# Layer-1 output products as seven block products of eight, and GpSimd work in instructions of 256 columns

## The reference, cut to what matters

```
h = rmsnorm(x) * (1 + scale) + shift
u, z = split(h @ w_in)                       # 1024 -> 2 x 2048
mixed = einsum(mean over windows of u - u, w_grp) * pool_scale   # four groups of 512 channels
y = (mixed * silu(z)) @ w_out                # 2048 -> 1024
x = x + gate * y
```

## Time and profile before

| | us |
|---|---|
| three runs | 1632.49, 1634.61, 1634.99 |
| median | 1634.61 |
| profiled execution | 1636.07 |
| its span, first to last instruction | 1633.3 |

### The profile page before, as it was taken

How to read it: one execution, slowest core, us unless ns; L and a number is a source line. 1 busy time by engine, 2 the same in 40 slices (tenths; PEclk the granted TensorE clock), 3 DMA queues, 4 the chain that set the end, 5 groups by cost and what they waited for, 6 DMA issues and landing times.

```text
span 1633.3 us, 24914 instructions
## 1 busy us (share of the span) xinstructions
PE 1594.1 (98%) x9703; PEld 1483.3 (91%) x9703; DVE 832.8 (51%) x1314; ACT 457.9 (28%) x969; POOL 377.0 (23%) x385
## 2 busy tenths in 40 slices
PE   6999999999999999998999999999999999999996
PEld 4899999999999999997888898888998989989896
DVE  4653549354854466448424563245623456234565
ACT  4321112110211011124416404064140542214423
POOL 3021222121221112111314213042231331314310
PEclk8999999999999999998999999999999999999998
DMA  9512221221122212210202212012120231201312
GB/s 335 194 56 78 68 57 54 67 79 55 56 67 67 67 56 62 84 41 28 65 14 72 91 41 78 13 61 89 50 68 14 65 97 41 66 25 40 110 38 110
DMA packets 137544, 115.01 MB, mean 70 GB/s; under 512 B 6013, under 2 KB 120281, under 8 KB 137442
## 3 DMA queue, kind: packets, MB, share of 16 engines
q1 hardware_dynamic: 135616, 112.87, 22.4%
q10 hardware_dynamic: 1834, 0.74, 0.2%
HBM read 99.05 MB, written 15.00 MB: 70 GB/s over the span
## 4 chain that ended last, share of the span: by engine, by line
PE 94%; DVE 3%; SPq 1%; DMA 1%; ACT 1%; issue 0%; ACTq 0%; DVEq 0%
PE psA L587 40%; PE psB L587 29%; PE psB L1857 7%; PE psA L1857 4%; PE psB L1914 2%; PE psB L1931 2%; PE psB L1922 2%; PE psX L1951 1%; PE psX L1896 1%; DVE a_hi L675 1%; PE psB L1963 1%; DVE y_rows L1650 1%; PE psX L1764 1%; DMA ada<-in_ada_w 1%; PE psB L1964 0%
## 5 line engine op out<-in xcount | busy, mean ns | idle before, releaser
L355 POOL TENSOR_TENSOR w_lo<-stage,w_hi 128x1024 fp32r<-128x1024 f32 x100 | 249.5, 2495 | 884.8 <-ACT w_hi L350 884.8
L350 ACT ACTIVATE w_hi<-stage 128x1024 fp32r<-128x1024 f32 x100 | 107.0, 1070 | 426.5 <-PE psB L587 297.5
L587 PE MATMUL psA<-h_hi,w_hi 128*128 128x362 f32 (+1 forms) x864 | 210.9, 349 | 5.1 <-DVE h_lo L491 4.8
L587 PE MATMUL psA<-h_lo,w_hi 128*128 128x362 f32 (+1 forms) x864 | 193.8, 329 | 0.0
L587 PE MATMUL psA<-h_hi,w_lo 128*128 128x362 f32 (+1 forms) x864 | 193.6, 329 | 0.0
L587 PEld LDWEIGHTS psA<-h_hi,w_hi 128*128 128x128 f32 x864 | 151.8, 191 | 28.1 <-issue 22.3
L587 PEld LDWEIGHTS psA<-h_lo,w_hi 128*128 128x128 f32 x864 | 151.9, 190 | 0.0
L587 PEld LDWEIGHTS psA<-h_hi,w_lo 128*128 128x128 f32 x864 | 151.7, 190 | 0.0
L587 PE MATMUL psA<-a_hi,w_hi 128*128 128x362 f32 (+1 forms) x480 | 109.6, 334 | 2.5 <-DVE a_lo L678 1.3
L587 PE MATMUL psB<-h_hi,w_hi 128*128 128x362 f32 (+1 forms) x480 | 109.6, 331 | 0.0
L587 PE MATMUL psB<-h_hi,w_lo 128*128 128x362 f32 (+1 forms) x480 | 107.8, 327 | 0.0
(11 more groups left out here) (364 smaller groups left out, 2767.9 us busy)
## 6 DMA issues: line engine op xcount, KB each, us to landing
stage<-in_gla_w_in SPq DMA_DIRECT2D x40, 512.0 KB, 3.6
stage<-in_pool_w_in SPq DMA_DIRECT2D x32, 512.0 KB, 3.9
ada_stage<-in_ada_w SPq DMA_DIRECT2D x24, 512.0 KB, 4.0
ada<-in_ada_w SPq DMA_DIRECT2D x16, 512.0 KB, 7.8
stage<-in_pool_w_out SPq DMA_DIRECT2D x16, 512.0 KB, 3.3
v<-in_state_gla SPq DMA_DIRECT2D x32, 256.0 KB, 2.6
out_new_gla_sample<-v SPq DMA_DIRECT2D x32, 256.0 KB, 2.1
stage<-in_gla_w_out SPq DMA_DIRECT2D x16, 512.0 KB, 3.4
```

What stands on the lines that cost most here:

```text
L350: nc.scalar.activation(slot_hi(plan, j), stage[:, j % 2, :], ACT.Copy).then_inc(lay.hi_done, 1)
L355: nc.gpsimd.tensor_tensor(slot_lo(plan, j), stage[:, j % 2, :], slot_hi(plan, j).bitcast(f32), ALU.subtract).then_inc(lay.lo_done, 1)
L587: last = nc.tensor.matmul(ps[u][:, t, 0:width], weight(w[:, p, :], k), a[:, k, n0:n0 + width], start=(k == 0 and pas == 0), stop=(k == kt ...
```

## The change

A slot's output product is a product of blocks: two halves of the tokens (544 columns each, `H0` and `H1`), two pairs of input tiles, two output tiles. Eight block products before; the change makes them from seven (Winograd's form), for O23, O45 and O67 in groups 0 to 2 and O23 and O45 in group 3. O01, and O67 of group 3, stay as they are.

- TensorE (`project_seven`): seven products of 12 matmuls (2 input tiles x 3 passes x 2 column parts of 272). Four of them take mixed operands, and some accumulate onto the result of an earlier one: 1, 3, 5 and 7 in one PSUM region of two banks, 4 and 6 in another, 2 alone. VectorE reads a region between two products that add to it, so TensorE waits for these reads.
- VectorE (`sum_tiles`, `sums_low`, `add_seven`): per group, eight sums of 544-column tiles for the mixed activations, four of them ahead of the gating of the last tile and four behind it, and eight low parts of them; per slot, seven additions of PSUM to `xT` in place of two.
- ScalarE (`sums_high`, `weights_high`): eight high parts of the sums per group, and four of 256 columns of the mixed weights per slot. Three of the sums' high parts stand ahead of the last silu.
- GpSimd (`weights_mixed`): per slot four mixed weight quarters, made in place in `stage`, and their four low parts, each of 256 columns in two strips of 128. Every low part of a slot, in both layers, is now four instructions of 256 columns in place of one of 1024. The low part of O23 waits until all activations of O01 are split (`act_part`).
- Loads: as `stage` is now read and rewritten after a slot's low part is done, O67's load waits for O23's product, and the first two loads of the next group for O45's and O67's. The mixed weights' high parts lie in `ada_stage`, so the load of the first adaLN columns of groups 1 to 3 moves behind that of slot 1. The mixed activations lie in `oT` (low), `PQ`, `G` and `SZ` (high).
- Ends: ScalarE's and GpSimd's loops end one group earlier and the last group is written out. The squares for the norm of layer 2 wait until O45 of group 3 is done, and the small weight copy `w_gl_hl` moves behind six of the seven whole squares.
- A few semaphores are merged (`ident_ready`, `copied`, `gate_ready`, the halves of `ada0_loaded` from the third on).

```diff
         def lo_slots(lay, plan, eng, g, j):
             eng.wait_ge(lay.hi_done, g * plan.slots + j + 1)
-            nc.gpsimd.tensor_tensor(slot_lo(plan, j), stage[:, j % 2, :], slot_hi(plan, j).bitcast(f32),
-                                    ALU.subtract).then_inc(lay.lo_done, 1)
+            if plan is PP and PP.names[j] == "O23":
+                eng.wait_ge(act_part, g * 3 + 3)
+            for n in range(0, D, D // 4):
+                c = slice(n, n + D // 4)
+                last = nc.gpsimd.tensor_tensor(slot_lo(plan, j)[:, c], stage[:, j % 2, c],
+                                               slot_hi(plan, j)[:, c].bitcast(f32), ALU.subtract)
+            last.then_inc(lay.lo_done, 1)
...
+        def project_seven(pe, g, name):
...
+            def multiply(out, i, h, mixed, a_high, a_low, first):
+                wh = mixed_quad(g, name, i, h) if mixed else quad(whi, i, h)
+                wl = quad(mlo if mixed else wlo, i, h)
+                for k in range(2):
+                    for pas, (w, x) in enumerate(((wh, a_high), (wh, a_low), (wl, a_high))):
+                        for n in range(2):
+                            last = nc.tensor.matmul(acc[out][n], w[:, k, :], x[:, k, n * (half // 2):(n + 1) * (half // 2)],
...
+            if name == "O23":
+                pe.wait_ge(L0.evac[0], g * PP.in_set[0] + PP.place[u] + 1)
...
+            slot_ready(pe, L0, PP, g, name)
+            multiply(a, 0, 0, False, a_hi[:, 0:2, H0], a_lo[:, 0:2, H0], True).then_inc(seventh_done, 1)
+            if name != "O23":
+                pe.wait_ge(seventh_read, read - 7 + 6)
+            multiply(b, 1, 0, False, a_hi[:, 2:4, H0], a_lo[:, 2:4, H0], True).then_inc(seventh_done, 1)
+            pe.wait_ge(mix_w_low, 8 * no + 5)
+            pe.wait_ge(mix_a_lo, 4 * g + 2)
+            pe.wait_ge(seventh_read, read + 1)
+            multiply(a, 1, 1, True, mix_a[1], alo[1], False).then_inc(seventh_done, 1)
...
+            pe.wait_ge(mix_w_low, 8 * no + 6)
+            multiply(c, 0, 0, True, mix_a[0], alo[0], True).then_inc(seventh_done, 1)
+            pe.wait_ge(mix_w_low, 8 * no + 7)
+            pe.wait_ge(mix_a_lo, 4 * g + 4)
+            pe.wait_ge(seventh_read, read + 3)
+            multiply(a, 0, 1, True, mix_a[2], alo[2], False).then_inc(seventh_done, 1)
+            pe.wait_ge(seventh_read, read + 4)
+            multiply(c, 1, 1, False, mix_a[3], alo[3], False).then_inc(seventh_done, 1)
+            pe.wait_ge(mix_w_low, 8 * no + 8)
+            pe.wait_ge(seventh_read, read + 5)
+            multiply(a, 1, 0, True, a_hi[:, 2:4, H1], a_lo[:, 2:4, H1], False).then_inc(L0.unit_done, 2)
...
+        def sum_tiles(dve, k, chain):
...
+            link(nc.vector.tensor_tensor(oT[:, 2 + k, H1], oT[:, k, H1], oT[:, 2 + k, H1], ALU.add))
+            nc.vector.tensor_tensor(oT[:, k, H1], oT[:, k, H0], oT[:, k, H1], ALU.subtract)
+            link(nc.vector.tensor_tensor(oT[:, k, H0], oT[:, 2 + k, H1], oT[:, k, H0], ALU.subtract))
+            nc.vector.tensor_tensor(oT[:, 2 + k, H0], oT[:, 2 + k, H0], oT[:, k, H0],
+                                    ALU.subtract).then_inc(mix_a_sum, 1)
+        mix_steps = {1: [(0, 0), (1, 0), (2, 0)], 2: [(0, 1), (1, 1)], 3: [(3, 0), (3, 1)], 4: [(2, 1)]}
...
+        def weights_mixed(pool, g, name):
...
+            pool.wait_ge(L0.lo_done, g * PP.slots + j + 3)
+            nc.gpsimd.tensor_tensor(quad(w, 0, 0), quad(w, 0, 1), quad(w, 0, 0), ALU.subtract).then_inc(mix_w_low, 1)
+            nc.gpsimd.tensor_tensor(quad(w, 0, 1), quad(w, 1, 1), quad(w, 0, 1), ALU.subtract).then_inc(mix_w_low, 1)
+            pool.wait_ge(mix_w_low, 8 * no + 2)
+            nc.gpsimd.tensor_tensor(quad(w, 1, 1), quad(w, 1, 1), quad(w, 0, 0), ALU.subtract).then_inc(mix_w_low, 1)
+            pool.wait_ge(mix_w_low, 8 * no + 3)
+            nc.gpsimd.tensor_tensor(quad(w, 1, 0), quad(w, 1, 0), quad(w, 1, 1), ALU.subtract).then_inc(mix_w_low, 1)
+            for n, (i, h) in enumerate(mix_order):
+                pool.wait_ge(mix_w_hi, 4 * no + n + 1)
+                nc.gpsimd.tensor_tensor(quad(mix_wl[:, j % 2, :], i, h), quad(w, i, h),
+                                        mixed_quad(g, name, i, h).bitcast(f32), ALU.subtract).then_inc(mix_w_low, 1)
...
+        def add_seven(dve, g, name, mod, chain, last_group):
...
+            dve.wait_ge(seventh_done, 6 * no + 1)
+            add_first(a, m).then_inc(seventh_read, 1)
...
+            add_first(b, m).then_inc(seventh_read, 1)
+            if name == "O23":
+                sums_low(dve, g, 4)
...
                     slot_free(L0, PP, g, j, sp)
+                    if j in (0, 1) and not first:
+                        wait_apart(sp, L0.unit_done, units(PP, g, 2 * j - 2))
+                    if j == PP.slot["O67"]:
+                        wait_apart(sp, L0.unit_done, units(PP, g, PP.unit["O23"] + 2))
...
+                    if name == "Z3":
+                        sums_high(act, g, 1)
                     if name[0] == "Z":
                         silu_out(act, L0, PP, g, int(name[1]))
                     if j + 2 < PP.slots:
                         split_slot(L0, PP, act, g, j + 2)
                     if j in extra:
                         extra[j]()
+                    if name == "Z3":
+                        for step in (2, 3, 4):
+                            sums_high(act, g, step)
+                        weights_high(act, g, "O23")
...
+            act.wait_ge(L0.unit_done, units(PP, NG, -2))
+            nc.scalar.activation(x_cols[:, NSUP + 1:NSUP + 2], eps[:], ACT.Sqrt)
+            squares_between(act)
             act.wait_ge(wgl_loaded, 16)
             nc.scalar.activation(w_gl_hl[:, :, 0:RANK], w_gl[:], ACT.Copy).then_inc(wgl_hi, 1)
-            nc.scalar.activation(x_cols[:, NSUP + 1:NSUP + 2], eps[:], ACT.Sqrt)
-            squares_between(act)
             squares_last(act)
...
                         gate_tile(dve, L0, PP, g, i, chain)
-                for name in ("O01", "O23", "O45"):
-                    add_branch(dve, L0, PP, g, name, mods[0], chain, last_group)
+                    if i == KG - 2:
+                        sum_tiles(dve, 0, chain)
+                        sums_low(dve, g, 1)
+                sum_tiles(dve, 1, chain)
+                add_branch(dve, L0, PP, g, "O01", mods[0], chain, last_group, (0,))
+                sums_low(dve, g, 2)
+                sums_low(dve, g, 3)
+                add_branch(dve, L0, PP, g, "O01", mods[0], chain, last_group, (1,))
+                add_seven(dve, g, "O23", mods[0], chain, last_group)
+                add_seven(dve, g, "O45", mods[0], chain, last_group)
```

More of the change, by code:

```diff
@@ L603, in w4, with quad, sevens, seven_no @@
             return lambda w, k: w[:, k * 256 + half * P:k * 256 + half * P + P]
+        def quad(w, i, h):
+            return w.rearrange("p (k h m) -> p k h m", k=KG, h=2)[:, 2 * i:2 * i + 2, h, :]
+        def sevens(g):
+            return ("O23", "O45") if isinstance(g, int) and g == NG - 1 else ("O23", "O45", "O67")
+        def seven_no(g, name):
+            return g * 3 + ("O23", "O45", "O67").index(name)
+        def seven_acc(g, name):
+            if isinstance(g, int) and g == NG - 1:
+                return {"O23": (1, 0, 2), "O45": (2, 0, 1)}[name]
+            return {"O23": (0, 1, 2), "O45": (1, 2, 0), "O67": (2, 0, 1)}[name]
@@ new lines, in mixed_quad @@
+        def mixed_quad(g, name, i, h):
+            last_group = isinstance(g, int) and g == NG - 1
+            return mix_w5[1 if name == "O45" and not last_group else 0][:, i, :, h, :]
+        def project_seven(pe, g, name):
+            u, p, no = PP.unit[name], PP.slot[name] % 2, seven_no(g, name)
+            a, b, c = seven_acc(g, name)
+            read = 7 * no
+            whi, wlo = w_hi[:, p, :], w_lo[:, p, :]
+            mlo, alo = mix_wl[:, p, :], mix_al
+            def multiply(out, i, h, mixed, a_high, a_low, first):
[5 more added lines that the diff above has]
+                            last = nc.tensor.matmul(acc[out][n], w[:, k, :], x[:, k, n * (half // 2):(n + 1) * (half // 2)],
+                                                    start=(first and k == 0 and pas == 0), stop=(k == 1 and pas == 2),
+                                                    skip_group_check=True)
+                return last
+            if name == "O23":
+                pe.wait_ge(L0.evac[0], g * PP.in_set[0] + PP.place[u] + 1)
+            else:
+                pe.wait_ge(seventh_read, read - 7 + (6 if seven_acc(g, name) == (2, 0, 1) and g == NG - 1 else 2))
+            slot_ready(pe, L0, PP, g, name)
[8 more added lines that the diff above has]
+            if name == "O23":
+                pe.wait_ge(L0.evac[1], g * PP.in_set[1] + PP.place[u + 1] + 1)
+            else:
+                pe.wait_ge(seventh_read, read)
+            pe.wait_ge(mix_w_low, 8 * no + 6)
[9 more added lines that the diff above has]
```

(29 more changed lines are left out.)

156 lines of the change are left out of this document (135 added, 21 removed).

## The result

The changed kernel takes 1641.46 us in the median of six runs (1638.05 to 1642.83), the kernel before 1634.40 in six (1632.49 to 1635.18): a ratio of 1.0043, interval 1.0032 to 1.0053. It is **7.1 us slower**; 9.4 us faster had been forecast. The profiled execution took 1638.93 us with a span of 1637.1, so 3.8 us of span more than before.

The account below looks back on a forecast made before the run. TensorE, busy 98% of the span, was taken as the bound. Gains of 15.9 and 4.4 less losses of 10.0 and 0.9 gave 9.4 us: median 1625.2 us, own range 1619 to 1631, 8 in 10 within 1614 to 1636.

Parts of the forecast that it names:

- Part 1: TensorE in eleven output slots: seven products of 272-column matmuls, slot 10.49 us against 11.93; 15.9 us gained.
- Part 2: Gating of the last tile: GpSimd held back, VectorE's conversion falls from 2.58 to 0.35 us; 4.4 us gained.
- Part 3: VectorE between O01 and product 3 of O23: TensorE stalls 2.5 us in each of four groups; 10.0 us lost.
- six meetings of ten: Between O01 and product 3: six of ten two-SBUF-operand VectorE instructions find a GpSimd piece in flight, about 0.55 us each.
- the 0.8 of room: VectorE's slack before product 3 of O23 without meetings: 0.2 us at the end and 0.6 idle before.
- Rival (b): In front of product 3 the granted clock falls in the stall: four falls, 6.8 us, 1632; chance 0.17.
- (d): Strict alternation of VectorE and GpSimd before product 3: stall 4.7 us a group, 8.8 more, 1634; chance 0.10.
- Rival (c): GpSimd becomes the bound from gating's end to U0, at 1.2 us a piece: slower, 1646; chance 0.09.
- Part 4: Rest of a slot: VectorE's reads, ScalarE's copies and GpSimd's other slots find cover; nothing gained or lost.
- Some 8 us ahead: GpSimd's other slots, 0.5 us longer each in pieces, were to end this far ahead of TensorE.
- Part 5: Weights that load later (O67, next group's U0): 8.3 us from slot end, under 10.5; nothing lost.
- part 6: End of layer 1: squares start behind O45's end and finish late; about 0.9 us lost, 0 to 2.

Follow-up runs that it names:

- e7: Changed kernel without the wait that holds GpSimd's low part of O23 until O01's activations are split: 1636.05 us, ratio 1.0016.
- e3: Changed kernel with 32 more matmuls of 240 columns behind product 2 of O23, into an unused bank, filling the stall: 1632.25 us, ratio 0.9995.
- e4: Changed kernel with O23 as eight products again, so only O45 and O67 run as seven, none in group 3: 1624.58 us, ratio 0.9948.
- e11: Changed kernel with every low part of a weight slot as one GpSimd instruction of 1024 columns, mixed weights still in pieces: 1635.81 us, ratio 1.0008.
- e5: Changed kernel with three of VectorE's eight low parts of the sums moved behind the read that releases product 3 of O23: 1629.21 us, ratio 0.9974.
- e6: Changed kernel with GpSimd's low part of O23 held until VectorE's four sums behind the gating are done: 1625.00 us, ratio 0.9939.
- e9: Changed kernel with O23's GpSimd low part held for the four sums and three sums' low parts behind product 3's releasing read: 1624.72 us, ratio 0.9946.
- e10: As e9, with the low parts of U0 to U3 as one GpSimd instruction of 1024 columns each: 1622.87 us, ratio 0.9928.

## Why the prediction was wrong

**Part 1 (right).** Pairs of 272-column matmuls start 0.25 us apart, 0.125 each (0.1243 forecast, bounds 0.1215 to 0.127). The slots without the stall are 10.61 on average, 10.49 forecast.

**Part 2 (right as far as it went).** O01's first half is 6.07 us instead of 7.17 in every group: 1.1 x 4, as forecast, and the work ahead of the gating fitted. That the held GpSimd work must then fall on the sums was in the prediction; that not holding it would have been cheaper was not (e7).

**Part 3 (the step that failed).** The place, the wait and the mechanism were right: product 3, VectorE as releaser, its row behind GpSimd's pieces. The term that was mis-sized is what the meetings cost: "I take six meetings of ten", 3.3 us in all. All ten met a piece, and that made 4.7 us in group 1. The four sums took 4.8 us (2.9 counted), the four low parts 4.75 (2.7), the two halves of O01 2.3 and 2.1 (1.8 each). A meeting cost 0.47 us, less than the 0.55 counted, so it is the number that was wrong. Short pauses and a slower read added 0.4; the 0.8 of room came off, and another 0.4 because TensorE arrived later than counted: 3.9 us in group 1. Over the four groups the gap was 3.3 to 4.1 us instead of 2.5, which is 15.2 us and not 10.0. The reason given for six, that GpSimd waits for ScalarE between its later pieces, did not hold: it waited 0.34 us in front of the mixed low parts, because its own slower pieces (1.07 instead of 0.73) had used the time up. Where it is earlier, it does wait: 3.85 us in e7.

The Trainium skill (SBUF — State Buffer, "Who interferes with whom") has the shared port pair as an exclusive lock, from which the prediction worked out strict alternation, and the trace agrees: 0.72 becomes 1.14 to 1.26. It says too that a VectorE instruction with at most one SBUF input, outside the two-port modes, does not contend, and the reads of PSUM agree: three of them take 1.52 us in the changed kernel, as before.

**Rival (b), which was given 0.17, came with (d), given 0.10.** They were priced as alternatives, each at 1632 to 1634, and both came. The forecast itself put the clock at nothing ("the granted clock whole in it"), on the ground that a gap of 0.64 us behind full products had no fall; the gap that came was six times as long. This is the second step that failed. The two are not independent: in the changed kernel the fall came in or right behind the gap, in groups 1 to 3, where it is 3.9 to 4.1 us, and not in group 0, where it is 3.3. Half of the 13.65 us at the lower level is 6.8; e3 shows 5.2 of it in the O23 slots. Both rivals added to the forecast make 1640.8, close to the 1641.46 measured, but that is partly luck: the gaps came 3.6 us below (d) and the clock 1.6 below (b), and small waits that neither counts filled the place. Of the Trainium skill's remark (TensorE: Matmul & The Clock Gate, "A second HAM failure mode: psum-queue depth-cycling"), cited in the prediction, the trace shows the fall behind a wait between PSUM regions; in the seven slots without a long gap there was none.

**Rival (c) (did not come).** The 40 pieces of group 1 took 0.83 us on average, under the 0.97 given as the limit: most of them met nothing. No U0 of a later group started late, and the U and Z stages take as long as before (125.05 us a group).

**Part 4 (wrong in one place).** "Some 8 us ahead" held for group 1's slots and not for U2 of group 0, whose low part before ended 0.1 us ahead of TensorE's start on it. This is TensorE's timeline of the changed kernel there:

```profile
75.91 0.43 PE L1984 MATMUL psA<-ident,hist 120*128 120x120 f32 x1 [1.61 <-issue]
```

1.4 us lost. The GLA stage gained 0.6.

**Part 5 (right), part 6 (wrong, small).** No later load shows as a wait. From the first matmul behind O67 of group 3 to GLA's first product it took 11.44 us, 11.58 before: nothing lost, 0.9 forecast.

**The sum again.** The eleven slots take 138.3 us, where parts 1 and 3 had 125.4: 13 us off, which covers the error of the profiled run, 12.2 (1626.7 forecast for a run like it, 1638.93 measured). 5.2 of it are longer gaps, 5.2 the clock, the rest small waits behind the gap and 0.12 a slot in the other seven. The start (1.1 worse, by single profiles whose starts differ by more), GLA, the layer's end and the tail (0.8 worse) nearly cancel out.

## What to carry to other kernels

When VectorE and GpSimd both have instructions queued that read SBUF, count a meeting for every one of VectorE's with two SBUF operands (here ten of ten), not a share of them, and give the pieces of GpSimd that are met the same delay; then look where the chain of waits can afford it, since the same work cost 4 us a group in front of a wait of TensorE and nothing one slot away (e4). A stall that TensorE did not have is not priced by its length alone: ask what clock it gets behind it, and add the two, as they came together here. Before an instruction is split into pieces, look for the one place in the kernel where it has no slack.

## What the runs showed of the hardware that was not expected

- The granted clock fell in or behind stalls of 2.73 us and more between full products, in groups 1 to 3 of the changed kernel, e7 and e11, and in none of the gaps of 1.8 us or less (e5, e6, e9, e10). In between it was not the length alone: 2.64 us (e7, group 0) and 3.27 us (the changed kernel, group 0) had no fall, 2.88 us (e11, group 0) had one. What decides there is open.
- With both queues full a piece of 256 columns on GpSimd took 1.07 to 1.11 us instead of 0.73, and a 544-column instruction on VectorE 1.14 to 1.26 instead of 0.72: a meeting costs both engines some 0.4 us.
- A VectorE conversion with one SBUF operand meets GpSimd as well: 0.77 instead of 0.35 us in e7, as the 2.58 us one did in the earlier trace rows. Whether it ran in one of the two-port modes, no trace here shows.
